# A 256-token long convolution moved to half-odd frequencies, its tokens split by parity, with the pool projection ahead of the inverse transform

## The reference, cut to what matters

```python
u = dwconv3(h @ w_in[:, 0:1536]); x0, x1, v = split(u)      # 256 tokens x 512 columns each
zv = x1 * v
k  = concat([h_fwd, 0, h_bwd[:0:-1]])                        # filter of 512 taps, from positions alone
y  = irfft(rfft(zv, n=512) * rfft(k, n=512))[:256]
y_hy = x0 * (y + zv * bias)
```

## Time and profile before

| | us |
|---|---|
| median of three executions | 1872.04 |
| the profiled execution | 1871.56 |
| its span, first to last instruction | 1869.4 |
| TensorE busy (matmul) | 1701.3 (91%) |
| VectorE busy | 466.2 (25%) |
| ScalarE busy | 259.3 (14%) |
| GpSimd busy | 23.8 (1%) |
| mean granted TensorE clock | 0.958 of full |

### The profile page before, as it was taken

One profiled execution on the slowest core, in us unless ns is written; L12 is line 12 of the kernel. 1 busy time (PEld: TensorE's weight loads), 2 busy tenths in 40 slices (PEclk: granted clock), 3 DMA queues, 4 the chain that ended last, 5 costly groups with the idle time before them and its releaser, 6 DMA issues.

```text
span 1869.4 us, 18922 instructions
## 1 busy us (share of the span) xinstructions
PE 1701.3 (91%) x8236; PEld 1153.3 (62%) x8236; DVE 466.2 (25%) x983; ACT 259.3 (14%) x572; POOL 23.8 (1%) x45
## 2 busy tenths in 40 slices
PE   7999998567667876799999999999999999999998
PEld 6485854222112321586788778874786888698853
DVE  4323103312111210334420322210325221222201
ACT  2222211000000000113220021100113210111100
POOL 0010000000000000000000000000000000000000
PEclk9999998888887997799999999999999999999999
DMA  8422747999999999733224424343433143344160
GB/s 340 171 95 86 292 158 275 426 429 429 431 429 431 429 430 382 331 135 135 90 90 158 179 91 180 136 198 114 181 141 130 51 161 127 139 177 168 63 242 23
DMA packets 31697, 405.24 MB, mean 217 GB/s; under 512 B 3520, under 2 KB 3840, under 8 KB 7168
## 3 DMA queue, kind: packets, MB, share of 16 engines
q1 hardware_dynamic: 31040, 401.03, 53.1%
q10 hardware_dynamic: 576, 3.01, 0.4%
HBM read 402.98 MB, written 1.05 MB: 216 GB/s over the span
## 4 chain that ended last, share of the span: by engine, by line
PE 77%; DMA 20%; DVE 1%; ACT 0%; issue 0%; POOL 0%; DVEq 0%; SPq 0%; ACTq 0%
PE bank L1055 76%; DMA w<-in_w_experts 10%; DMA zone<-in_w_experts 9%; PE bank L1099 1%; DMA w<-in_w_first 0%; ACT zone L1512 0%; DVE zone L2160 0%; POOL stat L2801 0%; DVE zone L1703 0%; ACT zone L1521 0%; DVE zone L2175 0%; ACT zone L1494 0%; DVE zone L2112 0%; DVE x L2120 0%; DVE x L1712 0%
## 5 line engine op out<-in xcount | busy, mean ns | idle before, releaser
L1055 PE MATMUL bank<-zone,w 128*128 128x256 f32 (+1 forms) x4224 | 813.2, 355 | 6.2 <-DMA w<-in_w_first 2.5
L1055 PEld LDWEIGHTS bank<-zone,w 128*128 128x128 f32 x4224 | 725.8, 192 | 95.2 <-issue 7.5
L1055 PE MATMUL bank<-w,zone 128*128 128x512 f32 (+1 forms) x1760 | 523.9, 653 | 68.8 <-DMA w<-in_w_experts 63.2
L1055 PEld LDWEIGHTS bank<-w,zone 128*128 128x128 f32 (+1 forms) x1760 | 202.2, 157 | 366.6 <-issue 280.8
L1055 PE MATMUL bank<-zone 128*32 128x512 f32 (+10 forms) x1912 | 326.2, 501 | 67.9 <-DMA zone<-in_w_experts 47.9
L1055 PEld LDWEIGHTS bank<-zone 128*128 128x128 f32 (+2 forms) x1912 | 183.4, 168 | 212.8 <-issue 124.3
L1521 ACT ACTIVATE zone<-bank 128x512 f32<-128x512 f32 (+2 forms) x129 | 72.3, 573 | 741.4 <-PE bank L1055 563.9
L2594 DVE TENSOR_SCALAR zone<-zone,vec 128x256 f32<-128x256 f32 x68 | 28.1, 413 | 256.7 <-ACT zone L2451 256.7
L2451 ACT ACTIVATE zone<-bank 128x256 f32<-128x256 f32 x68 | 24.9, 384 | 320.7 <-PE bank L1055 320.7
L1099 PE MATMUL bank<-const,zone 128*128 128x128 f32 (+2 forms) x286 | 42.4, 292 | 16.5 <-DVE zone L1689 7.6
L2109 DVE TENSOR_TENSOR zone<-zone,bank 128x512 f32<-128x512 f32 x8 | 5.5, 688 | 203.3 <-PE bank L1055 203.3
(11 more groups left out here) (232 smaller groups left out, 497.9 us busy)
## 6 DMA issues: line engine op xcount, KB each, us to landing
w<-in_w_layers SPq DMA_DIRECT2D x68, 2048.0 KB, 7.9
w<-in_w_experts SPq DMA_DIRECT2D x52, 2048.0 KB, 27.5
zone<-in_w_experts SPq DMA_DIRECT2D x47, 2048.0 KB, 27.3
w<-in_w_first SPq DMA_DIRECT2D x16, 2048.0 KB, 8.7
w<-in_w_layers SPq DMA_DIRECT2D x6, 1024.0 KB, 5.1
zone<-in_row ACTq DMA_DIRECT2D x2, 1024.0 KB, 4.8
zone<-in_table SPq DMA_DIRECT2D x1, 1664.0 KB, 17.9
zone<-in_table SPq DMA_DIRECT2D x1, 1216.0 KB, 16.6
```

The costliest lines, as they stand in the source:

```text
L1055: return eng.matmul(out, lhsT, rhs, start=start, stop=stop, **kw_)
```

## The change

The transform uses the 256 frequencies k + 1/2 in place of 0 to 256. No frequency has a real-only value, so the Nyquist row, its table and the one-row copies go. Frequencies come in pairs f and 256 - f. For such a pair the even tokens have the same cosine and opposite sine, the odd tokens the opposite cosine and the same sine. So 128 frequencies are computed for the even and for the odd tokens apart (`zdft`, contraction 128), and sums and differences give both members of the pair. The inverse does the same backwards: even tokens from one pair of combined spectra, odd tokens from another, each output 128 tokens wide with two contractions of 128.

- TensorE: the `zt` transposes read every second token of `u`. Groups `z0` to `z3` have one matmul of 512 columns each in place of two. `pool` is moved between `g` and the wait on `Y`. `yi` has sixteen matmuls of 128 columns in place of sixteen of 256. `filter_dft` has eight matmuls in place of ten.
- ScalarE: copies `z1` and `z3` out of PSUM, ahead of the `g` copies. Before the exponentials it waits for `Y` and not for `yi`.
- VectorE: twenty operations of 128x512 make `Y` (four sums or differences, twice six for the products, four sums or differences) in place of twelve and two one-row copies. `Y` is moved from `qez` to `ot`. The evacuation of `yi` comes after `qe`, `ke` and `kdec`, and its access to tokens has a step of two elements.
- Tables: the filter's part shrinks from 2432 to 2304 columns, the rest from 3328 to 3072. All that lies behind the table in the big tile moves by 384 columns.

```diff
-_columns(TABLE, [("dft", 1024), ("nyq", 128), ("decay", 1024), ("zT", 256), ("sin0", 256), ("inv", 1024), ("band", 2048)])
-FILTER_TABLE = TABLE["sin0"][0]
+_columns(TABLE, [("kdft", 1024), ("decay", 1024), ("zT", 256), ("zdft", 512), ("inv", 512), ("band", 2048)])
+FILTER_TABLE = TABLE["zdft"][0]
...
-    freq = np.arange(T)
-    angle = 2 * np.pi * ((time[:, None] * freq[None, :]) % (2 * T)) / (2 * T)
-    cos, sin = np.cos(angle), np.sin(angle)
-    sign = np.where(time % 2 == 0, 1.0, -1.0)
-    dft = np.concatenate([cos, sin], 1)
-    put(TABLE, t, "dft", dft.reshape(TT, P, 2 * T).transpose(1, 0, 2).astype(f))
-    sin0 = sin[:, :P].copy()
-    sin0[:, 0] = sign
-    put(TABLE, t, "sin0", sin0.reshape(TT, P, P).transpose(1, 0, 2).astype(f))
-    nyq = np.zeros((P, P))
-    nyq[:, 0] = sign[:P]
-    put(TABLE, t, "nyq", nyq.astype(f))
-    weight = np.full(T, 2.0) / (2 * T)
-    weight[0] = 1.0 / (2 * T)
-    inv = np.concatenate([cos.T * weight[:, None], sin.T * weight[:, None]], 0)
-    inv[T] = sign / (2 * T)
-    put(TABLE, t, "inv", inv.reshape(4, P, T).transpose(1, 0, 2).astype(f))
+    freq = np.arange(P) + 0.5
+    angle = 2 * np.pi * time[:, None] * freq[None, :] / (2 * T)
+    other = 2 * np.pi * time[:, None] * (T - freq)[None, :] / (2 * T)
+    kdft = np.concatenate([np.cos(angle), np.cos(other), np.sin(angle), np.sin(other)], 1)
+    put(TABLE, t, "kdft", kdft.reshape(TT, P, 4 * P).transpose(1, 0, 2).astype(f))
+    put(TABLE, t, "zdft", np.concatenate([np.cos(angle[0::2]), np.cos(angle[1::2]), np.sin(angle[0::2]), np.sin(angle[1::2])], 1).astype(f))
+    inv = np.concatenate([np.cos(angle[0::2]).T, np.cos(angle[1::2]).T, np.sin(angle[0::2]).T, np.sin(angle[1::2]).T], 1) / T
+    put(TABLE, t, "inv", inv.astype(f))
...
         def filter_dft(pl, i):
 
-            for f in range(2):
-                group(pl, f"k{i}{f}", [((P, 0, 512), [(dft[:, k, f * P:(f + 1) * P], hp_[:, k, :]) for k in range(TT)])])
-            for f in range(2):
-                parts = [(dft[:, k, T + f * P:T + (f + 1) * P], hm_[:, k, :]) for k in range(TT)]
-                if f == 0:
-                    parts += [(tv("nyq"), hp_[:, k, :]) for k in range(TT)]
-                group(pl, f"k{i}{2 + f}", [((P, 0, 512), parts)])
+            for j in range(4):
+                side = hp_ if j < 2 else hm_
+                group(pl, f"k{i}{j}", [((P, 0, 512), [(kdft[:, k, j * P:(j + 1) * P], side[:, k, :]) for k in range(TT)])])
...
-    Y = qez.rearrange("p (k d) -> p k d", k=4)
+    ysum = qez.rearrange("p (k d) -> p k d", k=4)
+    yprod = kez.rearrange("p (k d) -> p k d", k=4)
+    Y = ot.rearrange("p t d -> p (t d)").rearrange("p (k d) -> p k d", k=4)
     zt = kez[:, 0:1024].rearrange("p (t d) -> p t d", t=TT)
-    ya, yb = kez[:, 1024:1536], kez[:, 1536:2048]
...
-            transposes(pl, f"zt{t}", [(P, c * P, P, u[:, 8 + c, t * P:(t + 1) * P], ident) for c in range(4)])
+            transposes(pl, f"zt{t}", [(P, c * P, P, u[:, 8 + c, :].rearrange("p (s e) -> p e s", e=2)[:, t, :], ident) for c in range(4)])
...
-        for f in range(2):
-            group(pl, f"zc{f}", [((P, 0, 512), [(dft[:, k, f * P:(f + 1) * P], zt[:, k, :]) for k in range(TT)])])
-            group(pl, f"zs{f}", [((P, 0, 512), [((sin0[:, k, :] if f == 0 else dft[:, k, T + P:T + 2 * P]), zt[:, k, :])
-                                                for k in range(TT)])])
+        for k in range(4):
+            group(pl, f"z{k}", [((P, 0, 512), [(zdft[:, k, :], zt[:, k % 2, :])])])
         tall(pl, "g", hT, 4)
+        wide(pl, "pool", hT)
         eng.wait_ge(*pl.need(sem("Y"), 1))
         for g in range(2):
-            group(pl, f"yi{g}", [((P, j * T, T), [(Y[:, k, (2 * g + j) * P:(2 * g + j + 1) * P], inv[:, k, :]) for k in range(4)])
-                                 for j in range(2)])
-        wide(pl, "pool", hT)
+            group(pl, f"yi{g}", [((P, j * T + e * P, P), [(Y[:, k, (2 * g + j) * P:(2 * g + j + 1) * P], inv[:, k, :]) for k in (e, 2 + e)])
+                                 for j in range(2) for e in range(2)])
...
+        for k in (1, 3):
+            copy(pl, f"z{k}", ysum[:, k, :])
...
-        for g in range(2):
-            eng.wait_ge(*banks.filled_up(pl, f"yi{g}"))
+        eng.wait_ge(*pl.need(sem("Y"), 1))
...
-        for f in range(2):
-            eng.wait_ge(*banks.filled_up(pl, f"zc{f}"))
-            eng.wait_ge(*banks.filled_up(pl, f"zs{f}"))
-            zc, zs = banks.tile(pl, f"zc{f}"), banks.tile(pl, f"zs{f}")
-            kc, ks = Kf[layer][f], Kf[layer][2 + f]
-            yc, ys = Y[:, f, :], Y[:, 2 + f, :]
-            w(V.tensor_tensor(ya, zc, kc, ALU.mult))
-            w(V.tensor_tensor(yb, zs, ks, ALU.mult))
+        co, so = ysum[:, 1, :], ysum[:, 3, :]
+        for j, (even, odd, held) in enumerate((("z0", "z1", co), ("z2", "z3", so))):
+            eng.wait_ge(*banks.filled_up(pl, even))
+            for evacuated in banks.taken_up(pl, odd):
+                eng.wait_ge(*evacuated)
+            bank = banks.tile(pl, even)
+            w(V.tensor_tensor(Y[:, 2 * j, :], bank, held, ALU.add))
+            ins = V.tensor_tensor(Y[:, 2 * j + 1, :], *((bank, held) if j == 0 else (held, bank)), ALU.subtract)
+            ins.then_inc(*banks.done(pl, even))
+        for evacuated in banks.taken_up(pl, "z0", "z2"):
+            eng.wait_ge(*evacuated)
+        for s in range(2):
+            kc, ks = Kf[layer][s], Kf[layer][2 + s]
             eng.wait_ge(*pl.own(vstep))
-            v(pl, V.tensor_tensor(yc, ya, yb, ALU.subtract))
-            if f == 0:
-                v(pl, V.tensor_copy(yc[0:1, :], ya[0:1, :]))
-            V.tensor_tensor(ys, zc, ks, ALU.mult).then_inc(*banks.done(pl, f"zc{f}"))
-            V.tensor_tensor(ya, zs, kc, ALU.mult).then_inc(*banks.done(pl, f"zs{f}"))
-            for evacuated in banks.taken_up(pl, f"zc{f}", f"zs{f}"):
-                eng.wait_ge(*evacuated)
-            last = V.tensor_tensor(ys, ys, ya, ALU.add)
-            if f == 0:
-                v(pl, last)
-                v(pl, V.tensor_copy(ys[0:1, :], yb[0:1, :]))
-            else:
-                last.then_inc(*pl.up(sem("Y")))
-        for g in range(2):
-            eng.wait_ge(*banks.filled_up(pl, f"yi{g}"))
-            bank = banks.tile(pl, f"yi{g}")
-            for j in range(2):
-                c = 2 * g + j
-                ins = V.scalar_tensor_tensor(yh[:, c, :], zv[:, c * T:(c + 1) * T], pv(layer, "hy_bias", c), bank[:, j * T:(j + 1) * T],
-                                             ALU.mult, ALU.add)
-                w(ins) if j == 0 else ins.then_inc(*banks.done(pl, f"yi{g}"))
-        for evacuated in banks.taken_up(pl, "yi0", "yi1"):
-            eng.wait_ge(*evacuated)
-        eng.wait_ge(*pl.own(vstep))
-        yhf = yh.rearrange("p c t -> p (c t)")
-        V.scalar_tensor_tensor(yhf, yhf, 0.5, hz[:, 0:1024], ALU.mult, ALU.mult).then_inc(*pl.up(sem("yh")))
+            w(V.tensor_tensor(yprod[:, 0, :], Y[:, s, :], kc, ALU.mult))
+            w(V.tensor_tensor(yprod[:, 1, :], Y[:, 2 + s, :], ks, ALU.mult))
+            w(V.tensor_tensor(yprod[:, 2, :], Y[:, s, :], ks, ALU.mult))
+            v(pl, V.tensor_tensor(yprod[:, 3, :], Y[:, 2 + s, :], kc, ALU.mult))
+            w(V.tensor_tensor(ysum[:, s, :], yprod[:, 0, :], yprod[:, 1, :], ALU.subtract))
+            v(pl, V.tensor_tensor(ysum[:, 2 + s, :], yprod[:, 2, :], yprod[:, 3, :], ALU.add))
+        w(V.tensor_tensor(Y[:, 0, :], ysum[:, 0, :], ysum[:, 1, :], ALU.add))
+        w(V.tensor_tensor(Y[:, 1, :], ysum[:, 0, :], ysum[:, 1, :], ALU.subtract))
+        w(V.tensor_tensor(Y[:, 2, :], ysum[:, 2, :], ysum[:, 3, :], ALU.subtract))
+        V.tensor_tensor(Y[:, 3, :], ysum[:, 2, :], ysum[:, 3, :], ALU.add).then_inc(*pl.up(sem("Y")))
...
+        for g in range(2):
+            eng.wait_ge(*banks.filled_up(pl, f"yi{g}"))
+            bank = banks.tile(pl, f"yi{g}")
+            for j in range(2):
+                c = 2 * g + j
+                by = lambda a: a.rearrange("p (s e) -> p e s", e=2)
+                ins = V.scalar_tensor_tensor(by(yh[:, c, :]), by(zv[:, c * T:(c + 1) * T]), pv(layer, "hy_bias", c),
+                                             bank[:, j * T:(j + 1) * T].rearrange("p (e s) -> p e s", e=2), ALU.mult, ALU.add)
+                w(ins) if j == 0 else ins.then_inc(*banks.done(pl, f"yi{g}"))
+        for evacuated in banks.taken_up(pl, "yi0", "yi1"):
+            eng.wait_ge(*evacuated)
+        eng.wait_ge(*pl.own(vstep))
+        yhf = yh.rearrange("p c t -> p (c t)")
+        V.scalar_tensor_tensor(yhf, yhf, 0.5, hz[:, 0:1024], ALU.mult, ALU.mult).then_inc(*pl.up(sem("yh")))
```

More of the change, by code:

```diff
@@ L43 @@
 PI_MAX = 3.1415925
-ZONE = 35206
+ZONE = 34822
 GC = 64
@@ L365 @@
             'taken7': 14,
-            'vector_step': 119,
+            'vector_step': 127,
             'w_ready3': 144,
@@ L2232, in program @@
     w2f = [filt[:, 2 * HFO * i + HFO:2 * HFO * (i + 1)] for i in range(NL)]
```

(4 more changed lines are left out.)

## The result

The changed kernel took 1859.15 us (median of four executions, 1858.25 to 1860.89), the kernel before 1872.45 us on the same chip (four executions, 1871.66 to 1875.73). The ratio is 0.9927, with a 95% interval of 0.9910 to 0.9944. The forecast was 1858.3 us. The profiled execution of the changed kernel took 1860.89 us, the slowest of its four, with a span of 1859.1 us. TensorE's busy time fell from 1701.3 to 1684.8 us, VectorE's rose from 466.2 to 473.1 us. (In the changed file lines have moved: `group`'s matmuls stand at L1046, transposes at L1090.)

The account below looks back on a forecast made before the run. TensorE bounds the layers, DMA the experts. Forward -3.44 and inverse -3.34 give -6.78 a layer, -13.56 for both; with the table's -0.15, 1871.56 becomes 1857.9, and the median 0.5 above gives 1858.3 us (range 1856.5 to 1860.5).

Parts of the forecast that it names:

- Forward, -3.44 us a layer: Forward transform in each layer: half of its 16 records of 512 columns go, saving 3.44 of 6.88 us.
- Inverse, -3.34 us: Inverse (yi) in each layer: 32 records of 128 columns at 112 ns, 3.57 us in place of 6.91.
- rival B: In yi, 128-column products are held by weight loads and take as long as 256-column ones: 1865.0 us, chance 0.04.
- Transposes at 0: The eight zt transposes, 0.87 us, cost nothing more with a source of every second element; upper bound +0.87 us a layer.
- Y at 890.5, 14.8 us early: In layer0 VectorE completes Y at 890.5 us, 14.8 us before TensorE asks for it.
- Masks: VectorE's four score masks in layer0 end 5.3 us after gs starts against 4.5 today; un groups keep 2 us left.
- pool's 13.7 us is the cover: Pool ahead of yi replaces 7.8 us between Y and its use; without it TensorE asks 1 us after Y.
- Filter at 0: filter_dft in pass5 and pass6 loses four records each, hidden behind weight transfers: 0, other bound -3.5 us for both.
- The table's 0.15 us: The filter's table, 64 KB smaller inside the saturated DMA stretch, saves 0.15 us at 427 GB/s.
- One sign of being wrong: A last expert landing that moves by more than 0.2 us would show the prediction wrong.
- Rivals A: A wait at qke or an un bank, or slower zt transposes, takes 1 to 4 us a layer: 1860.5 to 1866, chance 0.10.
- D: TensorE stalls at qke and the clock drops from gs to un and go: +8 us a layer, 1888, chance 0.04.

## Why the prediction was right, step by step

- **TensorE bounds the layers and nothing else counts there: right.** Both windows stay full at clock 1.00, and in every kernel here TensorE's work, waits and slow records, added up, give the change of the layer stretch to within 0.4 us, while eight more sums on VectorE alone changed nothing.
- **Forward, -3.44 us a layer: right** (3.44 measured, 3.43 with that part alone).
- **Inverse, -3.34 us: right.** The gs row was the right neighbour; rival B is dead. The rule of the Trainium skill (TensorE: Matmul & The Clock Gate, section Back-to-back issue gap) would, by the estimate in the prediction, have made it -1.2; for these float32 records the measurement decides against that use of it.
- **Transposes at 0: off by 0.08 us a layer**, near the lower of its two bounds (0 and 0.87). The Trainium skill's 16-byte lines (SBUF — State Buffer, section Door 1: The DMA port swizzle) gave 0; the trace shows 10 ns more a transpose, a tenth of the upper bound. VectorE's strided evacuation kept its 0.87 us for two.
- **Y at 890.5, 14.8 us early: right.** In after's time, 3.18 us later than before's (863.74 against 860.56), that is 893.7; measured 893.48, with 15.0 us to spare. The first qke was due at 901.6 and came at 901.44.
- **Masks: the last ends 5.3 us after gs starts: 4.8 measured**, half of the difference since masks that wait for nothing start 0.6 us apart (the prediction has 0.69), half since the first one started 0.24 us earlier. The wait that I looked for at the un groups appeared only with twenty-five more sums.
- **"pool's 13.7 us is the cover": right, but not needed.** Y would have been 1 us early without it, as the text said, and pool behind yi costs nothing. The text did not say that the move alone does harm. Two other orders had to change with it. In the changed kernel the evacuation in its old place loses 14.4 us. In the old kernel the move alone loses 17 us, and there ScalarE's exponentials, which wait for yi, are what TensorE waits for. The change lets them wait for Y; no run puts that wait alone back.
- **Filter at 0: right,** with room for four times as much. **The table's 0.15 us was not seen:** from the issue of the table's load to the expert landing at 358.83 us (363.68 in the changed kernel) the fourteen traces take 47.8 to 48.5 us, a spread that hides it. **One sign of being wrong came up and means nothing:** the last expert landing moved from 740.18 to 745.04 us, far over the 0.2 us that the prediction allowed. But the shift stood already at the landing at 358.83 (363.68) us; from there to the last one it is 381.35 and 381.36 us, and 381.3 to 381.4 in every trace. The sign should have been a distance between two landings.
- **The sum:** -13.7 forecast, -13.4 in the layer stretch, -13.3 in the medians. The stretch is the test of the sum. That the medians come as close is in part luck: their interval reaches from 10.5 to 16.9 us, and they hold the 0.4 us outside the span and the spread of the regions ahead, which the sum doesn't have.
- **Rivals A and D did not come, but D's mechanism exists.** I priced the low level at 11.8 us a layer over a stretch of 23.7 us; a wait of 4.5 to 8.8 us costs 1.5 to 2.9 us beside itself, and less where a later signal holds TensorE anyway. What I had not seen is that it already comes with a single wait of 3 to 4.5 us in a stretch that is otherwise full. D would have needed 6.8 us of loss a layer; with the clock, a wait of about 4.5 us is enough for 6 to 7.5.

## What to carry to other kernels

Where one engine is full, count its records by shape, take their duration from a neighbour of the same shape, and the sum holds to a few tenths of a microsecond; then use the chain of the other engines only to check each wait, with the margin written down. When work is moved on one engine to cover a wait, list what the other engines have queued behind their own wait for the same data: here ScalarE's exponentials and VectorE's evacuation, both behind yi, decided over 17 and 14 us, more than the transform's 13. Before a slow record is given a price, see whether a later signal would have held the engine just as long. Compare kernels over a stretch that starts at a stamp inside the trace, when the regions ahead vary by more than the effect.

## What the runs showed of the hardware

A gap in a full TensorE stretch can cost more than itself. After waits of 4.46, 4.56, 6.02 and 8.82 us, in both layers of four kernels, the next records ran at a granted clock of 0.50, the 1.2 GHz level; after 3.1 us this came in one layer of two; after 2.28 us in neither. Where nothing else held TensorE (4.46 and 8.82 us) it cost 1.5 to 2.9 us beside the wait. Where the second qke came 3.53 us behind the first it cost 0.2 to 1.2 us (4.56 and 6.02 us) or nothing (3.1 us). A float32 transpose whose source has a step of two elements takes 119 ns in place of 109. Operations of VectorE on 128x512 that wait for nothing start 0.60 us apart at a duration of 0.69.
